# Moving the five buffers of moving operands of a 2,048-wide hybrid decoder kernel to five different places modulo 512 bytes

## The reference

```python
x = x + hybrid_mixer(x, ...)      # w_in (2048 x 7184), gated delta rule + attention, w_out
x = x + cross_attention(x, mem)   # 4 heads, 256 memory tokens
x = x + conv_ffn(x, ...)          # (silu(conv(h @ w_gate)) * (h @ w_up)) @ w_down, 5632 wide
x = rmsnorm(x)
x = layernorm(ALPHA * x + mamba2_mixer(x))        # a_w_in (2048 x 10304), scan, a_w_out
x = layernorm(ALPHA * x + sliding_window_attention(x))   # kv_w, b_w_in, b_w_out
```

## Time and profile before

| | us |
|---|---|
| median of 3 runs | 2648.81 |
| lowest, highest | 2643.33, 2649.91 |
| profiled execution | 2667.62 |
| its span, first to last instruction | 2665.8 |
| PE busy in it | 2538.2 (95%) |
| DVE busy | 1745.6 (65%) |
| ACT busy | 1204.4 (45%) |
| mean granted clock of PE | 0.982 |

### The profile page before, as it was taken

The page is one execution under the profiler, slowest core; times in us unless marked ns, Lnnn a source line. Parts: engine busy times, 40 slices in busy tenths (PEclk is TensorE's granted clock), DMA queues, the critical chain, the costliest instruction groups (busy, mean ns, idle before and its releaser), DMA issues.

```text
span 2665.8 us, 51914 instructions
## 1 busy us (share of the span) xinstructions
PE 2538.2 (95%) x21076; PEld 2459.1 (92%) x21076; DVE 1745.6 (65%) x2732; ACT 1204.4 (45%) x1878; POOL 352.9 (13%) x516
## 2 busy tenths in 40 slices
PE   7999999998799999999999999999999998899997
PEld 7999999988799999999999889999999988799896
DVE  6666645675566665665666677777677775466765
ACT  5333334443444444444444454445445443455553
POOL 1122210040110000000001101101101112210002
PEclk9999999999999999999999999999999999799998
DMA  5433335554355556556556554445454444344452
GB/s 210 143 112 111 111 106 176 172 174 141 112 167 187 186 169 206 186 168 204 189 167 186 166 169 153 159 154 177 153 181 143 158 140 138 110 147 148 143 166 87
DMA packets 124503, 418.37 MB, mean 157 GB/s; under 512 B 13796, under 2 KB 17644, under 8 KB 124012
## 3 DMA queue, kind: packets, MB, share of 16 engines
q1 hardware_dynamic: 124268, 415.06, 47.9%
HBM read 412.37 MB, written 3.68 MB: 156 GB/s over the span
## 4 chain that ended last, share of the span: by engine, by line
PE 73%; DVE 13%; ACT 7%; issue 5%; POOL 1%; DMA 1%; SPq 0%; ACTq 0%; DVEq 0%; POOLq 0%
PE b L690 22%; PE b L691 21%; PE b L692 21%; DVE WL L1521 4%; ACT WH L1146 3%; DVE t1s L1619 2%; PE b L805 1%; PE b L819 1%; ACT XH L1152 1%; PE b L1035 1%; PE b L662 1%; PE b L669 1%; PE b L816 1%; DMA t1s<-memT 1%; DVE XT L1702 1%
## 5 line engine op out<-in xcount | busy, mean ns | idle before, releaser
L1521 DVE TENSOR_TENSOR WL<-WR,WH 128x1024 fp32r<-128x1024 f32 (+2 forms) x811 | 967.0, 1195 | 502.2 <-ACT WH L1146 498.4
L690 PE MATMUL b<-XH,WH 128*128 128x256 f32 x4224 | 1218.0, 288 | 31.5 <-DVE WL L1521 23.6
L691 PE MATMUL b<-XL,WH 128*128 128x256 f32 x4224 | 1186.6, 281 | 0.0
L692 PE MATMUL b<-XH,WL 128*128 128x256 f32 x4224 | 1186.4, 281 | 0.0
L1146 ACT ACTIVATE WH<-WR 128x1024 fp32r<-128x1024 f32 (+2 forms) x811 | 811.1, 1010 | 510.2 <-PE b L692 504.8
L690 PEld LDWEIGHTS b<-XH,WH 128*128 128x128 f32 x4224 | 808.2, 191 | 49.7 <-issue 40.6
L691 PEld LDWEIGHTS b<-XL,WH 128*128 128x128 f32 x4224 | 803.5, 190 | 4.0 <-issue 3.3
L692 PEld LDWEIGHTS b<-XH,WL 128*128 128x128 f32 x4224 | 803.2, 190 | 0.0
L690 PE MATMUL b<-OH,WH 128*128 128x256 f32 x1680 | 482.8, 287 | 15.2 <-DVE XT L1702 11.7
L692 PE MATMUL b<-OH,WL 128*128 128x256 f32 x1680 | 471.3, 281 | 0.0
L691 PE MATMUL b<-OL,WH 128*128 128x256 f32 x1680 | 471.2, 280 | 0.0
(11 more groups left out here) (368 smaller groups left out, 2192.3 us busy)
## 6 DMA issues: line engine op xcount, KB each, us to landing
WR<-a_w_in SPq DMA_DIRECT2D x160, 512.0 KB, 3.6
WR<-w_in SPq DMA_DIRECT2D x112, 512.0 KB, 3.6
WR<-w_gate SPq DMA_DIRECT2D x88, 512.0 KB, 3.7
WR<-w_up SPq DMA_DIRECT2D x88, 512.0 KB, 3.6
WR<-a_w_out SPq DMA_DIRECT2D x64, 512.0 KB, 3.5
WR<-b_w_in SPq DMA_DIRECT2D x64, 512.0 KB, 3.8
WR<-w_down SPq DMA_DIRECT2D x64, 384.0 KB, 3.5
WR<-w_down SPq DMA_DIRECT2D x64, 320.0 KB, 3.1
```

The costliest lines, as they stand in the source:

```text
L690: mm(ps, WH[:, slot, at:at + P], xh, start=(k == 0), stop=False)
L691: mm(ps, WH[:, slot, at:at + P], xl, start=False, stop=False)
L692: m = mm(ps, WL[:, slot, at:at + P], xh, start=False, stop=(k == p["kt"] - 1))
L1521: dve.tensor_tensor(WL[:, s, 0:n], WR[:, r, 0:n], WH[:, s, 0:n].bitcast(F32), ALU.subtract).then_inc(*dve_w.up(i))
```

## The change

One pad of 48 floats (192 bytes) becomes five pads of 16, 16, 32, 16 and 16 floats (64, 64, 128, 64 and 64 bytes). Nothing else is changed: the same instructions in the same order on every engine.

```diff
     WR = sb("WR", [P, RAW, CK * P])
     WH = sb("WH", [P, HL, CK * P], F32R)
     WL = sb("WL", [P, HL, CK * P], F32R)
     XT = sb("XT", [P, 16, S])
-    sb("apart", [P, 48])
+    sb("apart0", [P, 16])
     XH = sb("XH", [P, 16, S], F32R)
+    sb("apart1", [P, 16])
     XL = sb("XL", [P, 16, S], F32R)
+    sb("apart2", [P, 32])
     OH = sb("OH", [P, 16, S], F32R)
+    sb("apart3", [P, 16])
     OL = sb("OL", [P, 16, S], F32R)
+    sb("apart4", [P, 16])
     with nc.sbuf_tensor("OX", [P, 12, S], F32R) as OX:
         pass
     t2x = sb("t2x", [P, 6, 512])
```

## The result

| | before | after |
|---|---|---|
| median, us | 2649.36 (4 executions) | 2694.73 (4 executions) |
| lowest, highest | 2643.33, 2672.99 | 2690.31, 2698.39 |
| profiled execution | 2667.62 | 2690.31 |
| ratio | | 1.0154, 95% interval 1.009 to 1.0218 |

The change makes the kernel slower: 45 us by the two medians, which is 1.7%, and 1.5% by the means, in which the one long execution of before counts too. One thing must be known to read these times. In all, the kernel before was executed 76 times besides the profiled one: 61 took 2636.8 to 2652.1 us, 15 took 2668.1 to 2677.9 us, and none lay between. The profiled execution of before, on which the prediction rested, took 2667.6 us, so it goes with the long ones.

The account below looks back on a forecast made before the run. PE's product stream of 18,432 matmuls was taken as the bound; only the feed-forward stage was to gain 13.5 us, all else zero, so 2648.8 - 13.5 = 2635.3 us, own range 2622 to 2645, full range 2600 to 2690.

Parts of the forecast that it names:

- the sign: Whole kernel: forecast 0.5% faster; chances faster 0.45, same 0.20, slower 0.35.
- The base: Whole kernel: profiled execution 2667.6 us, 18.8 us above the median, taken as constant, so 13.5 us came off 2648.8.
- about 0.3% (8 us): Whole kernel: the smallest difference from no change that a measurement was said to tell.
- The term that failed: Feed-forward stage: alternating places break up the slow phase, middle pace 115.6 ns, 6116 x 2.2 = 13.5 us less.
- I leave the mean as it is: Product stream outside the feed-forward stage: fast and slow stay mixed, mean 114.9 ns, no change.
- The bounds: Product stream: the trace's two paces bound the effect, 45 us gain if all fast, 36.1 us loss if slow.
- Rival 2: XH at 64 bytes, nearer the weights' place, slows stretches outside feed-forward to 117.8 ns: 36.1 us more, 2684.9 us; chance 0.33.
- Rival 1: Product stream: place doesn't matter or the allocator rounds the pads; 2648.8 us, 5 us either way; chance 0.17.
- the rule behind it: PE: two independent SBUF read ports, weight loads take nothing from the running matmul's reads, so the change is worth 0 us.
- Pads, ACT, DVE, POOL and DMA at no cost: Outside PE: pads untouched, same shapes at other 64-byte steps; zero, with 1 us either way.
- The steps differ by line in XH stretches: XH stretches: step from L690 to L691 not as long as from L691 to L692, where before all three agree.
- the load leaves little slack: Product stream: weight loads, 0.10 us each from rows 7, nearly fill the pace beside 256 moving columns, so small stalls show.

Follow-up runs that it names:

- 448 bytes: All five moving-operand buffers 448 bytes behind the weights, against the kernel before (192): median 2646.9 us, ratio 1.001.
- 176: All five moving-operand buffers 176 bytes behind the weights, against the kernel before (192): median 2648.9 us, ratio 1.002.
- the inserted matmuls: Kernel before with one small matmul, result not read, after every fourth w_up product of the feed-forward stage, 11 in all: 2661.0 us, ratio 1.006.
- 256 bytes: All five moving-operand buffers 256 bytes behind the weights, against the kernel before (192): median 2720.5 us, ratio 1.024.
- 320: All five moving-operand buffers 320 bytes behind the weights, against the kernel before (192): median 2690.6 us, ratio 1.014.
- the interleaving: WH and WL interleaved element by element, against the kernel before; all buffers at 128 bytes: 2743.6 us (1.034); at 0: 2730.6 us (1.029).
- the mixture of 192 and 448: Kernel before with XH, OL and OX at 192 bytes, XL and OH at 448: 2642.8 us, ratio 0.999.
- 0 bytes: All five moving-operand buffers 0 bytes behind the weights (no pad), against the kernel before (192): median 2718.8 us, ratio 1.023.
- 208: All five moving-operand buffers 208 bytes behind the weights, against the kernel before (192): median 2697.8 us, ratio 1.017.
- 224: All five moving-operand buffers 224 bytes behind the weights, against the kernel before (192): median 2697.1 us, ratio 1.018.

## Why the prediction was wrong

The measured 2694.7 us lies outside 2600 to 2690, and the sign was wrong.

**The base.** "That execution is 18.8 us above the median, which I take as constant." It was not constant: it was the feed-forward stage, locked in the slow pace for 730 us in that one execution. The prediction priced that at 6116 x 4.4 = 26.9 us, which is close to the distance between the two groups of times of the kernel before (means of 2644.8 and 2673.4 us, 29 us). At 448 bytes (the same place modulo 256) and at 176 the profiled execution fell into the fast pace there, 6,338 matmuls in the window instead of 6,116, and took 2642.0 us in the case of 448. So the usual execution has almost nothing to gain in that stage, and the forecast took 13.5 us off a median that already had that gain in it. No short execution of the kernel before was traced; this rests on the two kernels that share its pace, and on the inserted matmuls, which took the two groups away. With two groups 29 us apart, "about 0.3% (8 us)" was too fine as well: the intervals of the experiments are 0.2 to 1.1% wide on either side.

**The term that failed.** "so I expect that a phase that is bad for one isn't bad for the next, and take the middle of both paces, 115.6 ns." The XH stream measures 117.8 ns and the OH stream 119.2. Alternating places do put an end to the two paces, as argued, but the cycle that takes their place is a slow one; the high parts at 192 with the low parts at 64 did the same. The same step failed in the sentence after it, "I leave the mean as it is": outside the feed-forward stage the mean went from 114.9 to 118.1 ns, and 12,316 x 3.2 ns = 39 us, put at nothing, is most of the loss. No row could show where the cycle would settle. The bounds were wrong as well: they were the two paces of the trace, and the range allowed for a third only by a note that it was left out. Third paces, from 115 to 123 ns per step, are what most places have. Of the ten other places tried, 176 and 448 only equal 192.

**Rival 2 in size and reason.** It had the right side, at 0.33, and gave 2684.9 us with the stretches at 117.8 ns; the measured time is 10 us more. That it came so near is in part luck: added to the same median, it left out the 30 us that the feed-forward stage can lose when it was fast (6116 x 4.9 ns) and the 16 us that come back elsewhere (under "What held"), and one hid part of the other. Its reason, nearness of 64 bytes to the weights' place, is wrong: 256 bytes is slower than 64 and the same as 0, and 320 is as 64.

**Rival 1 and the rule behind it.** By the Trainium skill, "TensorE: Matmul & The Clock Gate", section "Step-by-step: what each phase is for", the two read ports of PE keep a weight load from taking anything from the running matmul. The runs disagree for this stream: moving only the weights by 64 bytes cost 65 us. The ports may be two, but the place of one operand against the other changes the rate. Nothing here tells what they share.

**What held.** Pads, ACT, DVE, POOL and DMA at no cost: DVE's busy time is 1745.5 us against 1745.6, the waits for WL 24.5 against 23.6 us. The steps differ by line in XH stretches, as was said they should. OX, which should have had a pace of its own, has steps of its own (118.3, 119.3 and 120.6 ns) with a mean of 119.4 beside 119.2. That the load leaves little slack held too, and more than was said: the weight loads of rows 7 were put at 0.10 us each, but the first two starts there are 0.026 us apart and the other six steps 0.112 us.

Matmuls are the currency: at 3.7 ns between the paces of the kernel after (118.2) and of the kernel at 448 bytes in its fast execution (114.5), some 17,650 undisturbed steps give 65 us, and the profiled executions are 48.3 us apart. Part of the difference is that the slower stream spends less time at the lower clock level: its mean granted clock is 0.986 against 0.983, so 2688 x 2 x 0.014 = 75 us at half rate against 2640 x 2 x 0.017 = 90 us, half of the difference, 7 us, regained. Another 9 us come back at the small steps of the mixers: PE's 314 steps from a product matmul to a small one take 99.6 us in all in the kernel after and 108.6 us at 448 bytes, and the difference is in those over 0.4 us, where PE waits (60.2 against 72.5 us). A stream that is slower comes later to small steps that wait for other engines, and waits less. With that all but 1 us is accounted for. The kernel with XH and XL alone moved shows the same: 101.7 us at these steps.

**What stays open.** Why a step takes what it takes, and why an inserted matmul turns one pace into the other. That the reads meet in the memory is only an idea; the one test of it that was made, the interleaving, went against the form in which it was put, and its floor of 112 ns left little to be seen. Why 192 is good and 64, 128 and 0 are not is measured and not explained. No version faster than the kernel before was found: the mixture of 192 and 448 is the same within its interval.

## What to carry to other kernels

When PE is busy all the time, count its matmuls per stretch before trusting its busy share: the same stream went at 113.3 or 117.8 ns here at one place of its buffers, and at 120.0 ns at another. Try the place of the moving operands against the weights in steps of 32 bytes over 256 bytes, one place for all, and look at the steps in the trace; don't reason it out and don't mix places. And before a profiled execution is used as a base, see whether its time belongs to the group of the median; if it doesn't, find the stretch that differs, or every price read from it is a price against the wrong kernel.

## What the runs showed that was not expected

- With 128 weight columns and 256 moving columns of 4 bytes at the 2.4 GHz level the best pace was 113.3 ns, 272 cycles; the pace at 0 and 256 bytes is 120.0 ns, 288 cycles; 256 cycles would be 106.7 ns. So 16 and 32 cycles on top of the columns. But weight loads with one moving column are 112 ns apart (L758 of before), so at the best pace most of the 16 may be the load's own time.
- At the 1.2 GHz level the steps were 0.21 us whatever the kernel's pace was at the other level: their mean is 209 ns before, after and at 0 bytes, with 213 ns the most frequent or nearly so. 256 cycles of 1.2 GHz are 213 ns, so nothing is seen on top.
- A stream can have two stable paces at one place and keep either over 6,000 matmuls, 6,338 against 6,116 in 720 us. Two small matmuls between products changed it eleven times of eleven. What decides which pace a stretch starts in is not shown.
- A place between multiples of 32 bytes acted as the next one up in the two cases tried (208 as 224, 176 as 192).
